# A hybrid decoder layer on one core: another order of the work at both stage borders

## The reference

```python
qa, ka, va, ga, hq, hk, hv, hg, gh = project(xp, norm_w, w_in, q_norm_w, k_norm_w, lb)
att = window_attention_prompt(qa, ka, va, sinks)   # window 128, 16 meta keys always seen, a sink per head
hgo, S_p = hgrn_prompt(hq, hk, hv, hg)             # S_t = diag(f_t) S_(t-1) + k_t v_t^T, o_t = S_t^T q_t
xp = xp + concat([att * silu(ga), rms_norm(hgo, hg_norm_w) * silu(gh)]) @ w_out
# the same for the 8 sample rows, whose keys, values and states come from the caches:
att = window_attention_sample(qa, ka, va, meta_k, meta_v, win_k, win_v, sinks)
```

## Time and profile before

| | |
|---|---|
| median of 3 runs | 1242.37 us (1241.58 to 1242.39) |
| profiled execution | 1239.61 us, of it 1237.8 us span |
| PE busy | 1182.3 us, 96% of the span |
| VectorE, ScalarE, GpSimd busy | 628.3, 396.2, 264.9 us |
| mean granted clock of TensorE | 0.975 of full speed |
| bytes moved | 104.07 MB, mean 84 GB/s |

### The profile page before, as it was taken

One profiled execution on the slowest core, in us unless ns is written; L12 is line 12 of the kernel. 1 busy time (PEld: TensorE's weight loads), 2 busy tenths in 40 slices (PEclk: granted clock), 3 DMA queues, 4 the chain that ended last, 5 costly groups with the idle time before them and its releaser, 6 DMA issues.

```text
span 1237.8 us, 25607 instructions
## 1 busy us (share of the span) xinstructions
PE 1182.3 (96%) x9462; PEld 974.5 (79%) x9462; DVE 628.3 (51%) x1687; ACT 396.2 (32%) x1178; POOL 264.9 (21%) x273
## 2 busy tenths in 40 slices
PE   6999999999999999996789999999999987999999
PEld 5777777877787777875658888888888866888887
DVE  6655555555555555555635555565666552222221
ACT  6311222222222222222215555555556552100010
POOL 0003333223332222322402232232232210000000
PEclk9999999999999999998869999999999988999999
DMA  7532111111111111144113311112112022243330
GB/s 266 177 115 85 61 60 59 54 50 48 53 47 55 58 59 59 44 170 167 44 53 141 116 68 59 42 42 77 52 43 78 18 77 81 102 153 124 130 137 37
DMA packets 47273, 104.07 MB, mean 84 GB/s; under 512 B 5024, under 2 KB 17824, under 8 KB 47200
## 3 DMA queue, kind: packets, MB, share of 16 engines
q1 hardware_dynamic: 47088, 103.28, 23.5%
q10 hardware_dynamic: 128, 0.03, 0.0%
HBM read 66.04 MB, written 38.26 MB: 84 GB/s over the span
## 4 chain that ended last, share of the span: by engine, by line
PE 87%; DVE 5%; ACT 3%; issue 3%; POOL 1%; DMA 1%; ACTq 0%; DVEq 0%; POOLq 0%; SPq 0%
PE h_bank_a L834 5%; PE h_bank_b L834 5%; PE o_bank L2102 5%; PE o_bank L2104 5%; PE o_bank L2103 5%; PE h_bank_b L836 5%; PE h_bank_b L835 5%; PE h_bank_a L836 5%; PE h_bank_a L835 5%; PE h_bank_t L818 3%; PE a_bank_a L1724 3%; PE a_bank_a L1725 3%; PE a_bank_b L1724 3%; PE a_bank_a L1726 3%; PE a_bank_b L1725 2%
## 5 line engine op out<-in xcount | busy, mean ns | idle before, releaser
L334 POOL TENSOR_TENSOR h_lv<-h_lv,h_tt 128x256 f32<-128x256 f32 x96 | 85.1, 887 | 274.3 <-PE h_near_a L860 92.4
L573 DVE TENSOR_TENSOR h_lv<-h_lv,h_tt 128x256 f32<-128x256 f32 x96 | 41.8, 436 | 147.4 <-PE h_near_a L860 66.5
L2102 PE MATMUL o_bank<-o_w_hi,o_m_hi 128*128 128x512 f32 x272 | 111.0, 408 | 3.2 <-DVE o_m_lo L2040 3.2
L2104 PE MATMUL o_bank<-o_w_hi,o_m_lo 128*128 128x512 f32 x272 | 107.8, 396 | 0.0
L2103 PE MATMUL o_bank<-o_w_lo,o_m_hi 128*128 128x512 f32 x272 | 107.3, 395 | 0.0
L834 PE MATMUL h_bank_b<-h_w_hi,h_h_hi 128*128 128x512 f32 x256 | 106.5, 416 | 0.1
L834 PE MATMUL h_bank_a<-h_w_hi,h_h_hi 128*128 128x512 f32 x256 | 106.1, 415 | 0.0
L1558 DVE CUSTOM_DVE_ANT_0 a_sm<-a_sc,a_hidden,a_neg_sink 128x272 f32<-128x272 f32 x128 | 59.1, 499 | 83.5 <-PE a_sc L1754 83.5
L836 PE MATMUL h_bank_b<-h_w_hi,h_h_lo 128*128 128x512 f32 x256 | 100.6, 393 | 0.0
L836 PE MATMUL h_bank_a<-h_w_hi,h_h_lo 128*128 128x512 f32 x256 | 100.4, 392 | 0.0
L835 PE MATMUL h_bank_b<-h_w_lo,h_h_hi 128*128 128x512 f32 x256 | 100.1, 391 | 0.0
(11 more groups left out here) (269 smaller groups left out, 2742.4 us busy)
## 6 DMA issues: line engine op xcount, KB each, us to landing
h_split<-h_h_hi SPq DMA_DIRECT2D x17, 512.0 KB, 3.3
h_split<-h_h_lo SPq DMA_DIRECT2D x17, 512.0 KB, 4.1
a_h_hi<-h_split SPq DMA_DIRECT2D x17, 512.0 KB, 3.5
a_h_lo<-h_split SPq DMA_DIRECT2D x17, 512.0 KB, 4.4
h_x<-x_prompt SPq DMA_DIRECT2D x16, 512.0 KB, 3.5
o_m<-mixed SPq DMA_DIRECT2D x16, 512.0 KB, 4.9
o_x<-x_prompt SPq DMA_DIRECT2D x16, 512.0 KB, 4.2
y_prompt<-o_y SPq DMA_DIRECT2D x16, 512.0 KB, 3.0
```

Source lines behind the costliest of these rows:

```text
L334: ins = pool.tensor_tensor(new[:, :, 0, :], old[:, :, 0, :], right.unsqueeze(2).to_broadcast([P, HW // (2 * b), b]), ALU.mult)
L2102: pe.matmul(out, hi, w_hi[a][:, k, :], start=(k == 0), stop=False)
L2104: ins = pe.matmul(out, lo, w_hi[a][:, k, :], start=False, stop=(k == KT - 1))
```

## The change

No arithmetic is changed. The change writes the instructions of both borders in another order, with other splits of loops, and moves some buffers.

In the recurrence, level 0 of each tile now stands behind both halves of the f projection, next to level 1:

```diff
                     pe.wait_ge(h_low, 2 * t1.n + 1)
                     project(t1, bank_a, 0, (0,))
-                level(t0, 0)
                 if ahead:
                     pe.wait_ge(h_low, 2 * t1.n + 2)
                     project(t1, bank_a, 0, (1,)).then_inc(f_proj, 1)
+                level(t0, 0)
                 level(t0, 1)
                 if tail:
```

The last iteration of the recurrence is written out and cut by `yield`, so that attention's kv weights are split within it, and q's and gate's in parts between the last tile's levels. On VectorE:

```diff
+            def split_weights(c, chunks=range(KT)):
+
+                for k in chunks:
                     dve.wait_ge(w_high, W_DONE + KT * c + k + 1)
                     dve.scalar_tensor_tensor(w_lo[c][:, k, :], raw[c][:, k, :], nw[:, k:k + 1], w_hi[c][:, k, :].bitcast(F32),
                                              ALU.mult, ALU.subtract).then_inc(w_ready, 1)
 
             split_weights(0)
             yield
-            dve.wait_ge(sink_loaded, 5 * 16)
+            split_weights(1, range(0, 5))
+            yield
             k_stats(tile(0, 0))
+            split_weights(1, range(5, 8))
+            dve.wait_ge(knw_loaded, 2 * 16)
             k_norm(tile(0, 0))
             place_v(tile(0, 0))
             dve.tensor_scalar(neg_sink[:, :], sink[:, :], -1.0, None, ALU.mult).then_inc(sink_negated, 1)
-            yield
-            split_weights(1)
             dve.wait_ge(sink_negated, 1)
+            yield
             k_stats(tile(0, 1))
             k_norm(tile(0, 1))
             yield
             q_stats(tile(0, 0))
             q_norm(tile(0, 0))
             yield
-            split_weights(2)
+            split_weights(2, range(0, 4))
+            yield
+            split_weights(2, range(4, 8))
```

On SP the kv weights are loaded earlier, tile 0's keys and values live in another buffer (`k_nat_0`, in g_exp) and six small transfers of them move here from ScalarE's queue:

```diff
             sp.wait_ge(before["f_proj"], TILES)
             load_weights(0)
+            yield
             sp.wait_ge(before["q_proj"], TILES)
...
+            sp.wait_ge(v_copied, 1)
+            sp.wait_ge(cache_loaded, 4 * 16)
+            sp.dma_start(KW[0:1, :, :], k_nat_0[s_rows, :]).then_inc(new_row, 16)
+            sp.dma_start(VW[0:1, :, :], v_nat_0[s_rows, :]).then_inc(new_row, 16)
+            sp.dma_start(new_win_k_sample[:, P - 1, :], k_nat_0[s_rows, :]).then_inc(meta_stored, 16)
+            sp.dma_start(new_win_v_sample[:, P - 1, :], v_nat_0[s_rows, :]).then_inc(meta_stored, 16)
+            sp.dma_start(new_meta_k, k_nat_0[0:META, :]).then_inc(meta_stored, 16)
+            sp.dma_start(new_meta_v, v_nat_0[0:META, :]).then_inc(meta_stored, 16)
             yield
             sp.wait_ge(v_placed, 1)
-            sp.wait_ge(buffers_zeroed, 1)
+            sp.wait_ge(buffers_zeroed, 2)
             for h in range(AH):
                 kv = h // (AH // KVH)
                 sp.dma_start(VMD[h * META:(h + 1) * META, h * HD:(h + 1) * HD], V_meta[:, kv * HD:(kv + 1) * HD]).then_inc(v_meta_spread, 16)
+            load_h(tile(0, 2))
+            yield
             sp.dma_start(new_win_k_sample[:, 0:P - 1, :], win_k[:, 1:P, :]).then_inc(rest_stored, 16)
             sp.dma_start(new_win_v_sample[:, 0:P - 1, :], win_v[:, 1:P, :]).then_inc(rest_stored, 16)
```

ScalarE's part of border 1:

```diff
             split_weights(0)
             yield
+            split_weights(1)
+            yield
+            split_weights(2, range(0, 4))
             keys_values(tile(0, 0))
-            yield
-
-            act.wait_ge(k_normed, 1)
-            act.wait_ge(v_copied, 1)
...
+            yield
             act.wait_ge(k_turned, 1)
             act.wait_ge(buffers_zeroed, 1)
             act.activation(KTS[:, :, :, 0:META], bank_t[:, :].rearrange("p (a b t) -> p a b t", a=KVH, b=2)[:, :, :, 0:META],
                            ACT.Copy).then_inc(k_placed, 1)
+            keys_values(tile(0, 1))
+            split_weights(2, range(6, 8))
+            square_q(tile(0, 0))
             place_k(tile(0, 1))
-            yield
-
+            square_q(tile(0, 1))
+            gate(tile(0, 0))
+            yield
+
```

On TensorE the first projections of attention are cut in halves, and the sample's attention goes into tile 1's iteration:

```diff
+            yield
+            project(t0, q_bank(t0), 1, range(4, 8), True).then_inc(q_proj, 1)
+            yield
+            pe.wait_ge(k_placed, 1)
+            turn_k(t1)
             pe.wait_ge(v_copied, 2)
-            project(t1, q_bank(t1), 1, range(KT)).then_inc(q_proj, 1)
+            project(t1, q_bank(t1), 1, range(0, 4))
+            yield
+            project(t1, q_bank(t1), 1, range(4, 8)).then_inc(q_proj, 1)
             yield
             pe.wait_ge(q_normed, 1)
-            project(t0, kv_bank(t0), 2, range(KT), True).then_inc(g_proj, 1)
+            project(t0, kv_bank(t0), 2, range(0, 4), True)
+            yield
+            project(t0, kv_bank(t0), 2, range(4, 8), True).then_inc(g_proj, 1)
             yield
             pe.wait_ge(q_normed, 2)
             project(t1, kv_bank(t1), 2, range(0, 4))
             yield
-            pe.wait_ge(k_placed, 1)
-            turn_k(t1)
             project(t1, kv_bank(t1), 2, range(4, 8)).then_inc(g_proj, 1)
-            yield
             pe.wait_ge(before["k_nat"], TILES)
             pe.wait_ge(q_done, 1)
-            pe.wait_ge(k_placed, 2)
             for g in range(4):
                 ins = pe.transpose(bank_t[:, g * P:(g + 1) * P], G[1][:, g * P:(g + 1) * P], ident[:, :])
             ins.then_inc(sq_turned, 1)
             pe.wait_ge(cache_loaded, 4 * 16)
             pe.wait_ge(new_row, 32)
+            pe.wait_ge(before["mix_done"], TILES)
...
             pe.wait_ge(sk_placed, 1)
             pe.wait_ge(sq_placed, 1)
             for b in range(NS):
                 ins = pe.matmul(sc[0:64, 0, 0:P + META], QZ[:, 64 * b:64 * b + 64], KTW[:, b, :], start=(b == 0), stop=(b == NS - 1))
             ins.then_inc(s_scored, 1)
-            pe.wait_ge(sq_placed, 1)
             turn_q(t1, 0)
+            project(t2, kv_bank(t2), 0, range(4, 8)).then_inc(kv_proj, 1)
+            pe.wait_ge(q_placed, 1)
+            turn_q(t1, 1)
+            pe.wait_ge(g_copied, 2)
+            project(t2, q_bank(t2), 1, range(0, 4))
             pe.wait_ge(s_exped, 1)
-            pe.wait_ge(g_copied, 1)
-            pe.wait_ge(before["mix_done"], TILES)
             pe.wait_ge(before["s_new"], TILES)
             pe.transpose(pt[:, 0, 0:64], s_p[:, 0:P], ident[0:64, 0:64])
             pe.transpose(pt[0:META, 0, 64:128], s_p[:, P:P + META], ident[0:64, 0:64]).then_inc(sp_turned, 1)
+            scores(t1, 0)
+            project(t2, q_bank(t2), 1, range(4, 8)).then_inc(q_proj, 1)
             pe.wait_ge(sp_placed, 1)
             for b in range(NS):
                 c = slice(64 * b, 64 * b + 64)
                 pe.matmul(bank_o[0:64, 0:KVH * HD], PZ[:, c], VW[:, b, :], start=(b == 0), stop=False)
                 ins = pe.matmul(bank_o[0:64, 0:KVH * HD], PZM[:, c], VM[:, b, :], start=False, stop=(b == NS - 1))
             ins.then_inc(s_pv, 1)
+            turn_p(t1, 0)
+            scores(t1, 1)
+            pe.wait_ge(k_normed, 3)
+            pe.wait_ge(v_copied, 3)
+            project(t2, kv_bank(t2), 2, range(0, 4))
             pe.wait_ge(v_meta_spread, AH * 16)
+            values(t1, 0)
+            turn_p(t1, 1)
+            scores(t1, 2)
+            values(t1, 1)
+            turn_p(t1, 2)
+            scores(t1, 3)
+            pe.wait_ge(q_placed, 2)
+            turn_k(t2)
+            project(t2, kv_bank(t2), 2, range(4, 8)).then_inc(g_proj, 1)
+            values(t1, 2)
+            turn_p(t1, 3)
+            pe.wait_ge(k_placed, 3)
+            turn_q(t2, 0)
```

At border 2 the last iteration but one of attention is written out too; the load of output rows waits for the kv projection of the last tile, the rows are turned within the tile in front, and the softmax steps of the last tile stand between groups of 12 output matmuls:

```diff
-            sp.wait_ge(g_proj, TILES)
+            sp.wait_ge(kv_proj, TILES)
             yield
             store_mixed(tile(0, TILES - 2))
+            yield
             store_mixed(tile(0, TILES - 1))
 
...
             for n in range(2):
                 load_mixed(tile(0, n))
+            for n in range(2):
                 load_x(tile(0, n))
             yield
-            with sp.Fori(0, ROWS // 2 - 1) as it:
+            load_mixed(tile(0, 2))
+            yield
...
 
             t0, t1 = tile(0, 0), tile(0, 1)
+            turn(t0, 0)
+            yield
+            turn(t0, 1)
+            yield
+            pe.wait_ge(w_ready, W_DONE + 2 * KT)
+            pe.wait_ge(attention["q_normed"], TILES)
+            multiply(t0, 0, range(0, 4))
+            yield
             pe.wait_ge(attention["q_placed"], 2 * (TILES - 1))
-            turn(t0, 0)
-            yield
-            turn(t0, 1)
-            yield
-            pe.wait_ge(w_ready, W_DONE + 2 * KT)
-            multiply(t0, 0, range(0, 4))
-            yield
+            turn(t1, 0)
             multiply(t0, 0, range(4, KT)).then_inc(multiplied, 1)
             yield
+            pe.wait_ge(attention["g_copied"], TILES)
+            turn(t1, 1)
             multiply(t0, 1, range(0, 4))
             yield
-            turn(t1, 0)
             multiply(t0, 1, range(4, KT)).then_inc(multiplied, 1)
             yield
-            turn(t1, 1)
             pe.wait_ge(attention["m_ready"], 4 * (TILES - 1))
-            iteration(t1, tile(0, 2))
+            multiply(t1, 0).then_inc(multiplied, 1)
+            yield
+            turn(tile(0, 2), 0)
```

(90 more changed lines are left out.)

292 lines of the change are left out of this document (190 added, 102 removed).

## The result

The changed kernel takes 1212.36 us (median of four, 1209.94 to 1214.57) against 1242.38 us (1241.58 to 1242.88): a ratio of 0.9764 with a 95% interval from 0.9748 to 0.978, 30.0 us less. Predicted were 1202 us, in a range from 1184 to 1224. The profiled execution was the slowest of the four: 1214.57 us with a span of 1212.7 us, 25 us less than that of before.

A forecast was written before the change was run, and what follows sets the result against it. TensorE bounds the kernel, losing time to waits and lower clock at two stage borders. Gains 23 + 15 + 2.5 = 40.5 us from 1239.61 give 1199.1; with the median 2.76 above the profiled run, 1202 us, range 1184 to 1224.

The forecast's parts named there:

- Level 0: Each HGRN iteration: placed next to level 1 it shares one matmul-size switch, gaining 2.5 us (-1 to 2.9).
- Border 1: First stage border: of at most 41.4 us, 18.3 us stay as idle and clock; gain 23 us (10 to 37).
- level 7: First border: TensorE waits 6.5 us (3 to 9) for VectorE's query row, behind 12.9 us of serial rows.
- the first probabilities: First border: tile 1's first transposes wait 3.5 us (3 to 5) for maxima behind the sample's result scaling.
- those after scores 2: First border: one 0.9 us set of value products covers 3.2 us before the transposes, leaving 2.3 us waiting.
- level 5 and the state product: First border: waits behind tile 0's query norm and the key copy, 2 us together (0 to 4).
- the clock: First border: slow matmuls behind two of the four new waits cost 4 us; the skill's rule would give 8.
- Border 2: Second stage border: earlier output-row loads and turning remove two waits and half-speed matmuls, gaining 15 us (0 to 22).
- A: Rival, both borders and recurrence: nearly all comes back as VectorE's row is in time; 1185 us, chance 0.2.
- B: Rival, first border: clock stays low for half of the work left there; 1220 us, chance 0.13.
- C: Rival, second border: output rows still late, the wait moves into tile 15, no gain there; 1217 us, chance 0.06.
- D: Rival: slower than before, 1.2 GHz up to the loop and again in the end tile; 1256 us, chance 0.04.

The follow-up runs named there:

- second profile: Changed kernel run again without any edit, with its own profile: 1212.32 us, profiled span 1208.2 us.
- m3: Changed kernel with the fourth tile's row load issued right behind the third's, ahead of the last tile's store: 1204.58 us.
- sp_late: Changed kernel with the third tile's row load put back behind the last tile's store: 1213.14 us.
- best: Changed kernel plus earlier fourth-tile load, earlier last query and key levels, earlier tile 1 value copy and maxima, tile 2's gate projection cut again: 1194.62 us.

## Why the prediction was right, and where its terms were off

The direction and the mechanism were right: both borders lost idle time and time at the lower clock, and level 0 gave its switch. The new time lies 10 us above the forecast, a gain of 30.0 instead of 40.4 us against the median. By terms:

- **Level 0**: 2.5 us forecast; 3.1 in the trace, about 2.3 by the medians. Right.
- **Border 1**: 23 us forecast, 14.9 found in the second profile, 11.6 in the first (16.5 + 9.1 left of 37.2). Three sizes were off. First, what there was to win: I took idle time plus the missing clock over the whole window, 41.4 us, called it a bound and then used it as the amount. Idle time at half clock was counted twice in it; read in steps of 1 us it is 22.2 + 15.0 = 37.2 us. That is 4.2 us of the miss. Second, the idle time that stays: 14.3 us forecast, 16.5 found. The four waits were the right ones: level 7 with 5.85 us (6.5 forecast), the first probabilities with 3.45 (3.5), those after scores 2 with 1.63 (2.3), level 5 and the state product with 0.66 and 1.89 (2 together). What I had not in the list are 1.70 us for the split of tile 0's keys, 0.98 before level 6 and smaller ones. Third, the clock: 4 us forecast for two of the waits, 5.5 to 9.1 found, in three to five places, one of which follows no wait. No run undoes the parts of border 1 one by one: that its gain comes of the split weights and of the sample's interleaved products rests on the waits that are gone and on the 0.51 that became 1.00.
- **Border 2**: 15 us forecast, 12.0 found. The failed step is "now that load is queued behind the first of the two, some 30 us before its rows are needed". It was true of the third tile in kind (issued at 996.15, turned at 1019.40 us without a wait, 23 us later), and I did not follow the next load in the same order, which stands, as before the change, behind the store of y and the load of x. It came late instead, and that is the DMA wait of several us that the prediction named as a sign of being wrong: 5.2 to 5.35 us, with 1.7 us of clock. m3 shows that this one place is worth 7.7 us, sp_late that without it the move of the third tile's load is worth 0.8 by the times and 3.0 by the table (12.0 less 9.0). So some 9 of the 12.0 us come of the rest of the change at this border, where I had put about two thirds of the gain on this one load.
- **Rivals**: A (1185 us) was not reached: level 7 did wait, and even best, with four of the remaining waits mended, lies at 1194.6. B happened in small: the clock did fall behind most waits, for some 4 us each, not for half of the stretch. C was the right kind of failure, at another tile. D had nothing for it.

The sentence on the Trainium skill ("TensorE: Matmul & The Clock Gate", section "HAM oscillation — how this bites in real kernels") put 8 us on the clock behind four waits, where I had counted 4. The two profiles have 5.5 and 9.1 us, and m3 and sp_late, which leave border 1 as it is, 6.7 and 6.6: all above my count, and on both sides of the rule's. But the rule speaks of bursts behind a pause, and the trace of best has a stretch at 0.57 in which TensorE was busy for 4.00 of 4.00 us, with the transposes of the sample's keys in front.

The level 7 chain was forecast at 12.9 us from the start of level 5; it took 579.94 to 593.65, 13.7 us. That the wait still came out 0.65 us shorter than forecast is two misses that cancel: TensorE's own work beside it took 7.8 us (580.08 to 587.86, a wait of 0.98 for level 6 in it) where I had 6.4.

The chain on VectorE:

```profile
579.94 4.13 DVE L1674 SCALAR_TENSOR_TENSOR a_w_lo<-a_raw,c_nw,a_w_hi 128x512 fp32r<-128x512 f32 x4
...
587.34 2.74 DVE L1674 SCALAR_TENSOR_TENSOR a_w_lo<-a_raw,c_nw,a_w_hi 128x512 fp32r<-128x512 f32 x4
...
592.63 0.69 DVE L1606 TENSOR_TENSOR a_q_nat<-a_bank_b,a_qrstd 128x512 f32<-128x512 f32 x1 [1.75 <-POOL a_qrstd L1325]
593.24 0.41 DVE L591 TENSOR_TENSOR h_lv<-h_lv,h_tt 128x256 f32<-128x256 f32 x1
```

## What to carry to other kernels

When a transfer's issue is moved ahead, follow the same queue one turn further: the next one takes its place as the late one unless it moves too. A wait that is removed uncovers the next row in the same chain on another engine (VectorE, then GpSimd, then ScalarE here), so look up all engines' rows behind a wait before pricing its removal. Sum idle time and lost clock from windows short enough that a window is either idle or at one clock; over a long window the two overlap.

## What the runs showed of the hardware

- The same program with the same waits had the full clock in one run and half of it in another, in stretches where TensorE was busy throughout (0.62 and 1.00 above): between two profiles 3.6 us at border 1 and 1.5 us at the start. The changed kernel's times run from 1209.45 to 1214.57 us, with mean granted clocks of 0.990 and 0.983 at these ends. What decides it was not found.
- Four low halves on VectorE took 4.13 us at 579.94 and 2.74 us at 587.34. The first time GpSimd was working through the weights of tile 0's queries, a level and four memsets, and the second time it was idle; that its work slows VectorE was not tried by itself.
